# Two heads at a time in a latent attention: values as weights side by side, probabilities scaled by a diagonal while they are turned, outputs laid out by features

## The reference, cut to what matters

```
def mla_attend(q, k, v):                      # q, k: (1, 8, L, 96), v: (1, 8, L, 64)
    s = einsum('bhqd,bhkd->bhqk', q_block, k) * 96 ** -0.5
    p = softmax(s, axis=-1)
    return einsum('bhqk,bhkv->bhqv', p, v)    # in blocks of 128 queries

att_l = mla_attend(q_latent, concat(k_latent, k_context), concat(v_latent, v_context))
att_c = mla_attend(q_context, k_context, v_context)
# then: concat([att, gla], features) @ w_out
```

## Time and profile before

| what | value |
|---|---|
| time, median of 3 runs | 3167.82 us (3163.91 to 3168.85) |
| the profiled execution: its time, its span | 3169.99 us, 3168.2 us |
| PE busy | 2843.3 us, 90% of the span |
| PEld busy | 2126.6 us, 67% |
| DVE busy, ACT busy | 1159.9 us (37%), 893.1 us (28%) |
| granted TensorE clock, mean | 0.949 of full speed |
| the attention units, first score matmul to last division | 1370.96 to 1503.63 us |
| the turn after them, first transpose to last copy | 1503.95 to 1507.18 us |

### The profile page before, as it was taken

One profiled execution on the slowest core, in us unless ns is written; L12 is line 12 of the kernel. 1 busy time (PEld: TensorE's weight loads), 2 busy tenths in 40 slices (PEclk: granted clock), 3 DMA queues, 4 the chain that ended last, 5 costly groups with the idle time before them and its releaser, 6 DMA issues. The chain is left out here.

```text
span 3168.2 us, 53190 instructions
## 1 busy us (share of the span) xinstructions
PE 2843.3 (90%) x23032; PEld 2126.6 (67%) x23032; DVE 1159.9 (37%) x1727; ACT 893.1 (28%) x1470; POOL 342.5 (11%) x287
## 2 busy tenths in 40 slices
PE   8987869999997998999899999998986777599999
PEld 6654644444444874657778888886865677478887
DVE  3133352222224306364343323323433344453343
ACT  3233321111112205234331212213343444342222
POOL 0010130000002402010100000010003444100001
PEclk9999889999998999999999999998987899899999
DMA  4259818999993111000222122112200000223221
GB/s 150 80 209 337 283 56 328 393 393 390 393 392 128 54 33 54 22 1 1 80 67 67 53 66 66 58 49 83 67 14 9 4 4 4 107 68 105 93 93 66
DMA packets 222636, 389.75 MB, mean 123 GB/s; under 512 B 9471, under 2 KB 99738, under 8 KB 221946
## 3 DMA queue, kind: packets, MB, share of 16 engines
q1 hardware_dynamic: 144938, 198.40, 18.3%
q10 hardware_dynamic: 77520, 188.75, 15.8%
HBM read 381.36 MB, written 5.77 MB: 122 GB/s over the span
## 5 line engine op out<-in xcount | busy, mean ns | idle before, releaser
L1958 PE MATMUL ps<-mlp_h_low,mlp_w_high 128*128 128x512 f32 (+1 forms) x768 | 272.0, 354 | 0.0
L1958 PE MATMUL ps<-mlp_h_high,mlp_w_high 128*128 128x512 f32 (+1 forms) x768 | 271.9, 354 | 0.0
L1958 PE MATMUL ps<-mlp_h_high,mlp_w_low 128*128 128x512 f32 (+1 forms) x768 | 271.6, 354 | 0.0
L1854 ACT ACTIVATE mlp_w_high<-mlp_ring 128x2048 fp32r<-128x2048 f32 x64 | 122.2, 1912 | 316.2 <-PE ps L1958 316.2
L1958 PE MATMUL ps<-mlp_x_low,mlp_w_high 128*128 128x512 f32 (+1 forms) x576 | 204.0, 354 | 0.0
L1958 PE MATMUL ps<-mlp_x_high,mlp_w_high 128*128 128x512 f32 (+1 forms) x576 | 203.9, 354 | 0.0
L1958 PE MATMUL ps<-mlp_x_high,mlp_w_low 128*128 128x512 f32 (+1 forms) x576 | 203.7, 354 | 0.0
L254 POOL TENSOR_TENSOR aT<-aT 128x512 f32<-128x512 f32 (+1 forms) x30 | 59.6, 1986 | 1180.2 <-ACT aT L246 1179.6
L1858 DVE TENSOR_TENSOR mlp_w_low<-mlp_ring,mlp_w_high 128x2048 fp32r<-128x2048 f32 x64 | 146.5, 2292 | 62.8 <-ACT mlp_w_high L1854 62.8
L1958 PEld LDWEIGHTS ps<-mlp_h_high,mlp_w_high 128*128 128x128 f32 x768 | 145.2, 189 | 20.4
L1958 PEld LDWEIGHTS ps<-mlp_h_high,mlp_w_low 128*128 128x128 f32 x768 | 145.2, 189 | 20.2
(11 more groups left out here) (558 smaller groups left out, 6009.4 us busy)
## 6 DMA issues: line engine op xcount, KB each, us to landing
mlp_ring<-in_mlp_w_dram SPq DMA_DIRECT2D x64, 1024.0 KB, 5.0
e_wg<-in_w_gate_dram ACTq DMA_DIRECT2D x15, 4096.0 KB, 15.4
e_wu<-in_w_up_dram ACTq DMA_DIRECT2D x15, 4096.0 KB, 15.1
ring<-in_w_down_dram ACTq DMA_DIRECT2D x15, 4096.0 KB, 13.7
ring<-in_ada_w_dram SPq DMA_DIRECT2D x24, 2048.0 KB, 9.6
ring<-in_w_in_dram SPq DMA_DIRECT2D x6, 2048.0 KB, 7.5
proj_ring<-in_even_w_in_dram SPq DMA_DIRECT2D x8, 1024.0 KB, 5.1
conv_ring<-in_gdn_w_in_dram SPq DMA_DIRECT2D x8, 1024.0 KB, 5.2
```

Source lines behind the costliest of these rows:

```text
L1854: act.activation(self.high[:, slot], self.ring[:, slot], ACT.Copy).then_inc(self.w_high, 1)
L1958: last = pe.matmul(bank(st, n, s, b - a), w[:, st % 2, k, n * P:(n + 1) * P], x[:, k, a:b], start=(k == 0 and p == 0), stop=(k == KT - 1 a ...
```

## The change

The order of the units becomes: pair of heads `j`, block `i`, head `h2` of the pair. For each unit DVE makes a diagonal matrix of the reciprocal row sums (`mla_diag`), and the turning of the probabilities becomes a plain float32 matmul with that diagonal as the moving operand in place of a transpose, so the turned probabilities come out divided. Each second step, the outputs of both heads of a pair are made in one go: 64 value columns are the weights, the turned probabilities (128 columns) move, and the two heads write PSUM partitions 0 to 63 and 64 to 127 of bank 6 (latent) or 7 (context). These outputs have features on the partitions; ACT copies a whole bank into `E.aT` once for each pair and kind. The division on DVE (line 2189), `O`, and the call of `turn` with its Block are removed. `mla_pT` doubles, since two heads' turned probabilities wait for the pair's product.

The diff, with the removed bodies cut (they stand above):

```diff
@@ -2089,105 +2089,116 @@
         gla_and_queries(E, X, cq, ckv, gq, gk, gv, gg, glow, qh, V, gate_dram)
         kh = sb("mla_k", [P, HEADS, TT])
         keys_and_gates(E, X, ckv, kpe, qh, kh, gg, gate_dram)
-        O = gg[:].rearrange("p q t -> p (q t)").rearrange("p (i n) -> p i n", n=512)
-        mla_units(E, qh, kh, V, O)
-        turn(E, "mla_oturn", [([O[:, i, k * P:(k + 1) * P] for i in ts], E.aT[:, k, ts[0] * P:(ts[-1] + 1) * P])
-                              for k in range(4) for ts in ((0, 1, 2, 3), (4, 5))])
-def mla_units(E, qh, kh, V, O):
+        mla_units(E, qh, kh, V)
+def mla_units(E, qh, kh, V):
     nc, sem = E.nc, E.sem
-    units = [(h, i, 0, TT) if i < 4 else (h, i, S, TT) for h in range(HEADS) for i in range(6)]
+    units = [(j, i, h2, 0 if i < 4 else S) for j in range(4) for i in range(6) for h2 in range(2)]
     n = len(units)
-    scored, maxed, exped, turned, evac_a, evac_v, summed, done = (
-        sem(f"mla_{x}") for x in ("scored", "maxed", "exped", "turned", "evac_a", "evac_v", "summed", "done"))
+    scored, maxed, exped, inverted, scaled, turned, evac_a, evac_v, summed, latent_out, ctx_out = (sem(f"mla_{x}") for x in (
+        "scored", "maxed", "exped", "inverted", "scaled", "turned", "evac_a", "evac_v", "summed", "latent_out", "ctx_out"))
     with ExitStack() as c:
         sb = lambda nm, s: c.enter_context(nc.sbuf_tensor(nm, s, FP))
-        pr, pT = sb("mla_pr", [P, 2, TT]), sb("mla_pT", [P, 2, TT])
+        pr, pT, diag = sb("mla_pr", [P, 2, TT]), sb("mla_pT", [P, 2, 2, TT]), sb("mla_diag", [P, 2, P])
         neg, tot, inv = (sb(x, [P, n]) for x in ("mla_neg", "mla_tot", "mla_inv"))
-        block = c.enter_context(nc.Block())
         score = lambda u, L: E.ps[:, (u % 2) * 2 * BANK:(u % 2) * 2 * BANK + L]
-        @block.tensor
-        def _(pe):
-            for t in range(n + 3):
-                if t < n:
-                    h, i, k0, k1 = units[t]
+        pair_sum = lambda w: pT[:, w % 2]
+        with nc.Block() as block:
+            @block.tensor
+            def _(pe):
+                for t in range(n + 4):
+                    if t < n:
+                        j, i, h2, k0 = units[t]
+                        if t >= 2:
+                            pe.wait_ge(exped, t - 1)
+                        for a in range(0, TT - k0, BANK):
+                            b = min(a + BANK, TT - k0)
+                            last = pe.matmul(score(t, b)[:, a:b], qh[0:QK, 2 * j + h2, i * P:(i + 1) * P], kh[0:QK, 2 * j + h2, k0 + a:k0 + b],
+                                             start=True, stop=True)
+                        last.then_inc(scored, 1)
+                    if 2 <= t <= n + 1:
+                        u = t - 2
+                        pe.wait_ge(scaled, u + 1)
+                        if u >= 1:
+                            pe.wait_ge(evac_a, u)
+                            pe.wait_ge(evac_v, u)
+                        for k in range((TT - units[u][3]) // P):
+                            last = pe.matmul(E.ps[:, 4 * BANK + k * P:4 * BANK + (k + 1) * P], pr[:, u % 2, k * P:(k + 1) * P], diag[:, u % 2, :],
+                                             start=True, stop=True)
+                        last.then_inc(turned, 1)
+                    if t >= 4 and t % 2 == 0:
+                        w = (t - 4) // 2
+                        j, i, _, k0 = units[2 * w]
+                        pe.wait_ge(evac_a, 2 * w + 2)
+                        pe.wait_ge(evac_v, 2 * w + 2)
+                        if i in (0, 4) and j >= 1:
+                            pe.wait_ge(ctx_out if i else latent_out, j)
+                        K = (TT - k0) // P
+                        for k in range(K):
+                            for h2 in range(2):
+                                h = 2 * j + h2
+                                last = pe.matmul(E.ps[64 * h2:64 * h2 + 64, 6 * BANK + i * P:6 * BANK + (i + 1) * P],
+                                                 V[:, k0 // P + k, h * 64:(h + 1) * 64], pair_sum(w)[:, h2, k * P:(k + 1) * P],
+                                                 start=(k == 0), stop=(k == K - 1), skip_group_check=True)
+                        last.then_inc(summed, 1)
+            @block.scalar
+            def _(act):
+                for t in range(n + 6):
+                    if t < n:
+                        L = TT - units[t][3]
+                        act.wait_ge(maxed, t + 1)
+                        if t >= 2:
+                            act.wait_ge(turned, t - 1)
+                        act.activation(pr[:, t % 2, 0:L], score(t, L), ACT.Exp, bias=neg[:, t:t + 1],
+                                       accum_out=tot[:, t:t + 1]).then_inc(exped, 1)
+                    if 2 <= t <= n + 1:
+                        u = t - 2
+                        L = min(BANK, TT - units[u][3])
+                        act.wait_ge(turned, u + 1)
+                        if u >= 4:
+                            act.wait_ge(summed, u // 2 - 1)
+                        act.activation(pair_sum(u // 2)[:, u % 2, 0:L], E.bank(4, L), ACT.Copy).then_inc(evac_a, 1)
+                    if t >= 6 and t % 2 == 0:
+                        w = (t - 6) // 2
+                        j, i = units[2 * w][0:2]
+                        if i == 3:
+                            act.wait_ge(summed, w + 1)
+                            act.activation(E.aT[:, j, 0:S], E.bank(6), ACT.Copy).then_inc(latent_out, 1)
+                        if i == 5:
+                            act.wait_ge(summed, w + 1)
+                            act.activation(E.aT[:, j, S:TT], E.bank(7, CTX), ACT.Copy).then_inc(ctx_out, 1)
+            @block.vector
+            def _(dve):
+                for t in range(n + 2):
+                    if t < n:
+                        dve.wait_ge(scored, t + 1)
+                        dve.tensor_reduce(neg[:, t:t + 1], score(t, TT - units[t][3]), AX.X, ALU.max, negate=True).then_inc(maxed, 1)
+                    if 1 <= t <= n:
+                        u = t - 1
+                        dve.wait_ge(exped, u + 1)
+                        dve.reciprocal(inv[:, u:u + 1], tot[:, u:u + 1]).then_inc(inverted, 1)
+                        dve.wait_ge(inverted, u + 1)
+                        if u >= 2:
+                            dve.wait_ge(turned, u - 1)
+                        dve.tensor_scalar(diag[:, u % 2, :], E.ident, inv[:, u:u + 1], None, ALU.mult).then_inc(scaled, 1)
                     if t >= 2:
...
+                        u = t - 2
+                        L = TT - units[u][3]
+                        dve.wait_ge(turned, u + 1)
+                        if u >= 4:
+                            dve.wait_ge(summed, u // 2 - 1)
+                        if L > BANK:
+                            dve.tensor_copy(pair_sum(u // 2)[:, u % 2, BANK:L], E.bank(5, L - BANK)).then_inc(evac_v, 1)
+                        else:
+                            dve.sem_inc(evac_v, 1)
```

More of the change, by code:

```diff
@@ L2109, in mla_units @@
         neg, tot, inv = (sb(x, [P, n]) for x in ("mla_neg", "mla_tot", "mla_inv"))
-        block = c.enter_context(nc.Block())
         score = lambda u, L: E.ps[:, (u % 2) * 2 * BANK:(u % 2) * 2 * BANK + L]
-        @block.tensor
-        def _(pe):
-            for t in range(n + 3):
-                if t < n:
-                    h, i, k0, k1 = units[t]
-                    if t >= 2:
[L2119 to L2190, removed]
```

## The result

The changed kernel takes 3180.81 us (median of 7 runs, 3169.33 to 3184.62), the kernel before 3168.42 in the same comparison (7 runs). The ratio is 1.0037, with a 95% interval of 1.0019 to 1.0054: slower by 0.37%, some 12 us.

What follows compares the result with a forecast made beforehand. PE's queue plus stalls was taken to bound the stage, with a loop through ACT second. Four pairs at +4.66 us, with the ends, gave +19.25; less 3.0 at the end, +16.2: forecast 3184 us, range 3175 to 3191.

Steps and rivals of the forecast that it cites:

- Turning by a diagonal: PE's turnings: twice the records, 12 per latent unit, holding PE 1.32 or 1.54 us, spanning 1.45 or 1.60.
- Paired outputs: PE's output products: two heads overlap at 0.054 us a record; latent pair 1.45 us against 2 x 1.28 before.
- rival B: Paired outputs do not overlap, 0.107 us a record: 24 us more, 3208 us; chance 0.05.
- The loop through ACT: Single turned buffer, ACT copy behind exponential: turning span plus 1.68 us, 3.13 at units 1, 3, 5; PE stalls.
- Rival A: The ACT loop costs nothing, turnings follow as fast as PE issues: 12.1 us less, 3172 us; chance 0.04.
- forecast of the profile: Changed profile: pair period near 37.4 us, PE idle about 0.46 at every odd latent unit, stage idle share about 10%.
- Even units, context units: Intervals between turnings: 4.34 us at units 2 and 4; 2.63, 1.82, 2.62, 2.56 at units 8 to 11.
- DVE hidden: DVE's reciprocal and diagonal, ready about 1.7 us after turning starts, fit the shortest 2.56 interval with 0.9 to spare.
- Rival D: Diagonal comes late on DVE, as with a 1 us self-wait: little added until 0.9 us is used up.
- The end: Last turning to last copy: 2.41 us against 5.42 before, giving back 3.0 us, removed turn included.
- Rival C: Diagonal product runs as one record per block: 22.8 us less with the ends, about 3161 us; chance 0.02.

Runs made afterwards that it cites:

- the run with transposes: Changed kernel with the turning done by identity transposes again, diagonals made but unused: stage 132.07 us against 154.34, median 3163.56 us.
- the unpaired order: Changed kernel with the paired output's loops exchanged, all key blocks of one head, then the other: stage 169.17 us against 154.34, median 3194.28 us.
- the run with the copy first: Changed kernel with ACT's copy of turned unit t-2 ahead of the exponential of unit t: stage 139.45 us against 154.34, median 3166.99 us.
- the kept turn: Changed kernel with the old turning stage put back behind it, results unused: stage 157.96 us against 154.34, one run 3207.57 us.

## Why the prediction was right

The forecast was 3184 us (3175 to 3191) and the median is 3180.81; slower was forecast with a chance of 0.92, and slower it is. Step by step, the stage:

- *Turning by a diagonal.* Spans of 1.45 and 1.60 were taken from the dilated attention; 1.50 and 1.58 were measured. They hold PE 1.34 and 1.51 (1434.78 to 1436.12, 1430.42 to 1431.93) against 1.32 and 1.54. The rows of another function priced the operation within 0.05 us, and the run with transposes shows that this one term carries the loss: 22.3 us.
- *Paired outputs.* 1.46 us (1431.93 to 1433.39) for 1.45. The overlap, rival B's subject, is real, and rival B falls: 24 records in 1.53 us are 0.054 a record. Its 24 us is the price with no overlap at all, which no run here measured; the unpaired order keeps the overlap where the heads meet, and its stage is 14.8 longer.
- *The loop through ACT.* 3.18 for 3.13 at odd units, 2.75 for 2.71 at unit 7. That PE would stall here was the step that could least be read from the kernel before, where the loop binds at few units; the exchange on ACT shows it as a cause. A pair of heads has PE busy for 34.06 of its 37.43 us, idle for 9%, where about 10% was forecast.
- *Rival A* was sized wrongly. It took 2.67 us for PE's products at unit 5, where the scores that follow are a context unit's, so they take 1.81. It gave 12.1 us for a loop that costs nothing; the run with the copy first measured 14.9. The sum itself did not use that figure, because there the loop decided. With the right figure, 3172 would have read about 3169. The same slip is in the forecast of the profile, 0.46 us idle at every odd latent unit: it is 0.38 after units 1 and 3, and 1.24 after unit 5.
- *Even units, context units.* 4.36 for 4.34 at units 2 and 4. Units 8 to 11 took 2.61, 1.74, 2.55 and 2.53 us for 2.63, 1.82, 2.62 and 2.56. A whole pair took 37.43 us (turnings of unit 1 at 1427.24 and 1464.67 in PE's timeline) for 37.36. That it is so close is in part luck: the latent units are 0.27 longer than forecast and the context units 0.20 shorter.
- *DVE hidden.* Right: the diagonal came 1.6 us early for the turning that follows an odd unit, and making each some 0.4 us later cost nothing. Rival D falls.
- *The end.* 3.54 us from the last turning to the transfer against 6.75 before, so 3.2 given back for 3.0; the kept turn alone is 3.6.
- *Rival C* falls: `x12` for six blocks.

From the first turning to the last the sum gave 145.05 us, and the trace 145.80 (1386.27 to 1532.07). The sum gave +16.2 for the stage, the trace +16.8. The medians differ by 12.4, with an interval of 0.19% to 0.54%, 6 to 17 us, and 16.8 lies inside it too. What the 4.4 between them is made of is not shown; the swings in the other stages are larger than that.

## What to carry to other kernels

Price a new operation by the same form elsewhere in the same trace, and then do a second sum: the loop through each single buffer, since an operation that becomes longer on one engine can make a wait on another engine's order bind. In such a loop put the operation that frees the buffer ahead of the one that only feeds it; here that took 14.9 us off the changed kernel's stage and 8.0 off that of the kernel before. To fold a scaling into a float32 transpose makes it a full product with two records a block. A scaling in place on an engine with room was cheaper by far here (122.0 us against 139.45, both with the copy first), and the pairing of heads was the part worth keeping.

## What the runs showed of the hardware that was not expected

Matmuls with 64 weight columns that write different halves of the partitions overlap when they alternate (24 records in 1.53 us, 0.054 a record, half of the 0.107 of records that write all partitions), and partly when they only meet: 12 of one head and then 12 of the other take 2.46 us, but four and four take 0.66 us, as long as when they alternate. In the group of 12 and 12 the eight records around the hand-over start 0.055 us apart and the others 0.109. That suggests a reach of about four records; no run varied it.
